# Final scaling of a two-layer encoder trunk: two of the last eight output tiles moved from VectorE to GpSimd

## The reference

```python
def _rmsnorm(x, g):
    xf = x.astype(jnp.float32)
    y = xf * lax.rsqrt(jnp.mean(xf * xf, axis=-1, keepdims=True) + EPS)
    return (y * g.astype(jnp.float32)).astype(x.dtype)
...
        x = x + gate * y
    return _rmsnorm(x, final_g)
```

## Time and profile before

| what | us |
|---|---|
| device time, median of 3 runs (805.86 to 807.53) | 806.22 |
| device time of the profiled execution | 806.58 |
| its span | 804.7 |
| PE busy in it | 793.3 (99%) |
| DVE busy | 654.6 (81%) |
| ACT busy | 459.7 (57%) |
| POOL busy | 86.6 (11%) |

### The profile page before, as it was taken

One profiled execution on the slowest core, in us unless ns is written; L12 is line 12 of the kernel. 1 busy time (PEld: TensorE's weight loads), 2 busy tenths in 40 slices (PEclk: granted clock), 3 DMA queues, 4 the chain that ended last, 5 costly groups with the idle time before them and its releaser, 6 DMA issues.

```text
span 804.7 us, 15186 instructions
## 1 busy us (share of the span) xinstructions
PE 793.3 (99%) x5562; PEld 743.9 (92%) x5562; DVE 654.6 (81%) x952; ACT 459.7 (57%) x642; POOL 86.6 (11%) x112
## 2 busy tenths in 40 slices
PE   8999999999999999999999999989999999999996
PEld 8879999999999999998889888789999999988896
DVE  5989999999999999898896698398888888883334
ACT  4675656565656565572323876656667777762220
POOL 1010000000000000102301242010000000000000
PEclk9999999999999999999999999999999999999999
DMA  9986566666666666679874794655555454454103
GB/s 347 372 205 187 150 183 182 183 182 183 182 182 182 182 182 183 184 262 349 307 236 101 266 223 85 144 149 151 146 156 151 121 145 143 144 182 184 53 1 105
DMA packets 42673, 146.02 MB, mean 181 GB/s; under 512 B 5400, under 2 KB 7702, under 8 KB 42640
## 3 DMA queue, kind: packets, MB, share of 16 engines
q1 hardware_dynamic: 31760, 111.16, 38.5%
q0 software_dynamic: 9728, 32.26, 21.8%
q10 hardware_dynamic: 1152, 2.18, 0.7%
HBM read 109.14 MB, written 4.21 MB: 141 GB/s over the span
## 4 chain that ended last, share of the span: by engine, by line
PE 89%; DMA 4%; DVE 3%; issue 2%; ACT 1%; SPq 0%; POOL 0%; POOLq 0%; DVEq 0%; ACTq 0%
PE pp L1362 11%; PE pp L1363 11%; PE pp L1364 11%; PE pp L1221 8%; PE pp L1222 7%; PE pp L1223 7%; PE p_aux L1362 7%; PE p_aux L1364 7%; PE p_aux L1363 7%; PE pp L1317 2%; PE pp L1494 2%; PE pp L1496 2%; PE pp L1495 2%; PE p_aux L1609 2%; DMA raw_s<-in_stream 1%
## 5 line engine op out<-in xcount | busy, mean ns | idle before, releaser
L1362 PE MATMUL pp<-h_hi,wh 128*128 128x256 f32 x280 | 79.3, 283 | 0.0
L1364 PE MATMUL pp<-h_hi,wl 128*128 128x256 f32 x280 | 79.2, 283 | 0.0
L1363 PE MATMUL pp<-h_lo,wh 128*128 128x256 f32 x280 | 79.2, 283 | 0.0
L826 ACT ACTIVATE wh<-wt 128x1024 fp32r<-128x1024 f32 x56 | 59.0, 1055 | 13.7 <-DVE wt L1899 7.6
L1918 DVE TENSOR_TENSOR wl<-wt,wh 128x1024 fp32r<-128x1024 f32 x56 | 66.5, 1219 | 0.2 <-ACT wh L826 0.2
L1362 PE MATMUL pp<-s_hi,wh 128*128 128x256 f32 x224 | 63.4, 283 | 0.0
L1363 PE MATMUL pp<-s_lo,wh 128*128 128x256 f32 x224 | 63.4, 283 | 0.0
L1364 PE MATMUL pp<-s_hi,wl 128*128 128x256 f32 x224 | 63.4, 283 | 0.0
L1364 PE MATMUL p_aux<-s_hi,wl 128*128 128x256 f32 x224 | 63.4, 283 | 0.0
L1362 PE MATMUL p_aux<-s_hi,wh 128*128 128x256 f32 x224 | 63.4, 283 | 0.0
L1363 PE MATMUL p_aux<-s_lo,wh 128*128 128x256 f32 x224 | 63.4, 283 | 0.0
(11 more groups left out here) (292 smaller groups left out, 2659.1 us busy)
## 6 DMA issues: line engine op xcount, KB each, us to landing
raw<-in_stream SPq DMA_DIRECT2D x140, 512.0 KB, 4.2
wl<-raw POOLq DMA_DIRECT2D x28, 512.0 KB, 4.5
raw_l<-in_stream SPq DMA_DIRECT2D x18, 512.0 KB, 5.9
raw_s<-in_stream SPq DMA_DIRECT2D x16, 512.0 KB, 13.6
wl_b<-raw POOLq DMA_DIRECT2D x16, 512.0 KB, 4.5
raw_m<-in_stream SPq DMA_DIRECT2D x14, 512.0 KB, 3.3
xv_lo<-y POOLq DMA_DIRECT2D x8, 512.0 KB, 6.1
x_s<-in_xt SPq DMA_DIRECT2D x4, 512.0 KB, 5.9
```

Source lines behind the costliest of these rows:

```text
L826: act.activation(wh[g % 2][:, at], wt[g % 2][:, at], ACT.Copy).then_inc(t_hi_cut, 1)
L1362: pe.matmul(out, hi, hi_of(k), start=fresh and k == 0, stop=False, skip_group_check=not fresh)
L1363: pe.matmul(out, hi, lo_of(k), start=False, stop=False, skip_group_check=not fresh)
L1364: mm = pe.matmul(out, lo, hi_of(k), start=False, stop=k == 3, skip_group_check=not fresh)
```

## The change

In the second half, tiles 4 and 5 are no longer scaled by VectorE.

- ScalarE multiplies the second half of tiles 4 and 5 by `final_g` right after `square_x(1, 2)`, in place (two new 128x256 instructions).
- TensorE makes a third broadcast in the second half, 256 columns in one, into another bank of PSUM (`p_pair[1]`). It is issued behind the two that VectorE reads.
- ScalarE copies that bank to SBUF (`rstd_end`), ahead of its stores.
- GpSimd multiplies the two weighted tiles by `rstd_end`, one instruction each.
- VectorE scales six tiles, 0, 1, 2, 3, 6 and 7. SyncE stores 0, 2, 6 and then 4, ScalarE 1, 3, 7 and then 5, still one store a tile.

```diff
+END_POOL = (4, 5)
+END_DVE = (0, 1, 2, 3, 6, 7)
...
+        rstd_end = at_kb("rstd_end", 60, [P, HALF])
...
         @block.sync
-            for k in range(0, KD, 2):
-                sp.wait_ge(out_ready, KD + k + 1)
-                sp.dma_start(out[:, k, halves[1]], x_b[:, k, halves[1]]).then_inc(out_sent, 16)
+            for n in range(0, len(END_DVE), 2):
+                sp.wait_ge(out_ready, KD + n + 1)
+                sp.dma_start(out[:, END_DVE[n], halves[1]], x_b[:, END_DVE[n], halves[1]]).then_inc(out_sent, 16)
+            sp.wait_ge(end_ready, 1)
+            sp.dma_start(out[:, END_POOL[0], halves[1]], x_b[:, END_POOL[0], halves[1]]).then_inc(out_sent, 16)
...
         @block.gpsimd
+            pool.wait_ge(end_weighed, len(END_POOL))
+            pool.wait_ge(end_copied, 1)
+            for n, k in enumerate(END_POOL):
+                pool.tensor_tensor(x_b[:, k, halves[1]], x_b[:, k, halves[1]], rstd_end[:, :], ALU.mult).then_inc(end_ready, 1)
...
         @block.scalar
                 square_x(1, j)
+                for k in range(2 * j, 2 * j + 2):
+                    if k in END_POOL:
+                        act.wait_ge(sq_ready, KD + SQUARES + k + 1)
+                        act.activation(x_b[:, k, halves[1]], x_b[:, k, halves[1]], ACT.Copy,
+                                       scale=cols[:, C_FG + k:C_FG + k + 1]).then_inc(end_weighed, 1)
             cut_hi_late(W_BOUT // 4 + DPAIRS - 1, 0, 1)
             square_half(1, 0)
             square_half(1, 1)
-            for k in range(1, KD, 2):
-                act.wait_ge(out_ready, KD + k + 1)
-                act.dma_start(out[:, k, halves[1]], x_b[:, k, halves[1]]).then_inc(out_sent, 16)
+            act.wait_ge(rstd_bc, 7)
+            act.activation(rstd_end[:, :], p_pair[1][:, 0:HALF], ACT.Copy).then_inc(end_copied, 1)
+            for n in range(1, len(END_DVE), 2):
+                act.wait_ge(out_ready, KD + n + 1)
+                act.dma_start(out[:, END_DVE[n], halves[1]], x_b[:, END_DVE[n], halves[1]]).then_inc(out_sent, 16)
+            act.wait_ge(end_ready, 2)
+            act.dma_start(out[:, END_POOL[1], halves[1]], x_b[:, END_POOL[1], halves[1]]).then_inc(out_sent, 16)
...
         @block.tensor
+            broadcast(p_pair[1][:, 0:HALF], 7, slice(HALF, S))
...
         @block.vector
-                for k in range(KD):
+                for k in range(KD) if half == 0 else END_DVE:
```

More of the change, by code:

```diff
@@ L311, in build @@
         dve_step = sem("dve_step")
+        end_weighed, end_copied, end_ready = sem("end_weighed"), sem("end_copied"), sem("end_ready")
         s_sum, s_hi_cut, s_cut = sem("s_sum"), sem("s_hi_cut"), sem("s_cut")
```

## The result

| what | before | after |
|---|---|---|
| device time, median (7 runs each) | 806.28 | 809.84 |
| lowest and highest run | 805.86 to 807.6 | 809.24 to 810.12 |
| ratio, 95% interval | | 1.0041 (1.003 to 1.0052) |
| profiled execution: device time, span | 806.58, 804.7 | 809.24, 807.4 |

A forecast was written before the change was run, and what follows sets the result against it. The prediction took VectorE's scalings and the DMA engines' stores, level in rate, to bound the last 6 us. Its terms, 0 + 0 + 0 - 0.1 us, took 806.58 to 806.5 profiled, 806.1 as a median; range 805.4 to 807.2.

The forecast's parts named there:

- third rival: Closing barrier: GpSimd's drain is fixed work after its last instruction, ending the kernel 3.3 us later, at 809.5; chance 6%.
- the sum (0 + 0 + 0 - 0.1 us): Whole kernel: weighting, broadcast and copy, and multiplies cost nothing; stores gain 0.1 us, so 806.58 becomes 806.5.
- the 0.3 us of the barrier: End of the kernel: the barrier takes 0.3 us of the 804.7 span after SyncE passes its wait at 804.4.
- The range: Device time from 805.4 to 807.2, said to take in all cases but the drain.
- Weighting: ScalarE behind the square at 772.03: two instructions, 0.84 us, delaying VectorE's cut but hidden by 3.9 us slack; cost nothing.
- a gap: TensorE near 779.7, where its fourth slot is due: a gap there would show the weighting not hidden.
- Broadcast and copy: Last stage: broadcast 799.07 to 799.66, ScalarE's copy 0.38 us to 800.08, fitting before its stores by 0.1 us; cost nothing.
- The multiplies: GpSimd in the last stage: two multiplies at 0.65 us each, 800.12 to 801.4.
- The second rival's exclusion: GpSimd and VectorE exclude each other in the last stage, last issue near 803.0; rival's size 0 to 0.5 us slower, 12%.
- The stores: End of the kernel: last issue moves from 802.52 to 802.1, 0.42 us earlier; 0.05 to 0.1 us of it arrives.
- they would have kept up: First rival, last stores: DMA engines keep up, so the end moves the whole 0.42 us, to 805.8; chance 17%.
- the forecast of no change: Whole kernel: median 806.1 against 806.22, 62% for the forecast; 91% that it measures the same.

The follow-up runs named there:

- E4: The changed kernel with the two multiplies made by VectorE, behind its six tiles, instead of GpSimd: 806.17, ratio 1.0003 to the kernel before.
- E3: The kernel before plus one late two-column memset on GpSimd that nothing waits for: 808.0, ratio 1.0022.
- E1: The changed kernel without GpSimd's drain in the closing barrier: 806.29, ratio 1.0007 to the kernel before.
- E2: The kernel before without GpSimd's drain in the closing barrier: 806.31, ratio 1.0005.
- E10: The changed kernel without GpSimd's drain, storing only 128 of 256 columns of each second-half tile: 805.71, ratio 0.9998 to the kernel before.

## Why the prediction was wrong, by its own steps

**The step that failed is the third rival's chance.** The price and the point from which it decides were right: 3.3 us forecast, 3.46 measured; POOL working past 798.2. I gave it 6% because "its end lies 0.1 us behind SyncE's release at 804.4, which would be a coincidence". It was one. The drain took 6.34 us after GpSimd's last instruction in the kernel before, in the changed one and in E4, 6.32 in E3, whatever SyncE did. In the sum (0 + 0 + 0 - 0.1 us) GpSimd's later end has no term: the 0.3 us of the barrier behind SyncE's wait were carried over, and the runs showed 3.87 us there in the changed kernel. A long sequencer instruction with no visible cause, on the very engine that the change gave new last work, deserved a case inside the range; one coincidence of 0.1 us was the whole argument for leaving it out. The range ended at 807.2, below the lowest run of 809.24.

**The rest held.**

- *Weighting.* VectorE's cut began 3.20 us after the update ahead of it (770.47 to 773.67) instead of 2.40 (771.24 to 773.64), so 0.80 us late for 0.84 forecast, and its idle time behind it shrank from 6.51 to 5.72. TensorE lost nothing by it: E1 is level with E2, and around 779.7, where the prediction looked for a gap, the starts of its matmuls in the changed kernel stay 0.12 us apart. The update before and after:

```profile
771.24 0.75 DVE L2097 SCALAR_TENSOR_TENSOR x_b<-pp,mod,x_b 128x512 f32<-128x512 f32 x1 [1.90 <-PE pp L1223]
```

```profile
770.47 0.75 DVE L2118 SCALAR_TENSOR_TENSOR x_b<-pp,mod,x_b 128x512 f32<-128x512 f32 x1 [1.90 <-PE pp L1243]
```

- *Broadcast and copy.* The copy started 0.43 us after the first scaling, as forecast (799.70 against 799.27), took 0.38, and ScalarE's first store went at 799.40, 0.90 after the first scaling; before it was also 0.90.
- *The multiplies* took 0.72 us each for 0.65 estimated. An estimate of 0.56 us came from the Trainium skill, GPSIMD Engine Reference, section Elementwise side-by-side cycle accounting; the row is longer.
- *The second rival's exclusion.* VectorE's six scalings took 2.44 us, still 0.39 apart, while both multiplies ran beside them. The Trainium skill, SBUF — State Buffer, section Who interferes with whom, says that a VectorE instruction with at most one input in SBUF does not contend with GpSimd: the trace agrees.
- *The stores.* Last issue 0.38 us earlier for 0.42; release 0.03 us earlier for 0.05 to 0.1. The queue after, over 9.9 us from 797.5:

```profile
out_t<-x_b SPq DMA_DIRECT2D x4, 128.0 KB, 1.9
out_t<-x_b ACTq DMA_DIRECT2D x4, 128.0 KB, 2.0
```

The median landing is now 1.9 us on SyncE's queue and 2.0 on ScalarE's instead of 1.8, and the last needs 2.2: what the issues gained, the full DMA engines took back, as their share and E10 show. The estimate from the Trainium skill, DMA: Bandwidth & Descriptors, section Why small descriptors are slow, by which they would have kept up, does not give the rate of these stores.

So with GpSimd's drain taken out (E1, 806.29) the forecast of no change is right, and for its reasons. No version here beats the kernel before: E1, E2 and E4 lie within 0.1% of it, and the last stage is bound by its stores.

## What to carry to other kernels

Before an engine is given new last work, look at what its sequencer still has to do after it: here GpSimd's drain ran 6.34 us beyond its last instruction, and in the kernel before it was hidden with only some 0.05 us to spare. Counted from the first scaling, GpSimd's last instruction ended 3.49 us later after the change, and the kernel 3.46 us later. Taking two tiles off VectorE gained 0.03 us here, since its product leaves through DMA engines that were already full at the same rate. And an instruction of unexplained length near the critical end belongs in the range, however neatly its end fits another event.

## What the runs showed that I had not expected

- GpSimd's drain at the end takes 0.1 us and, up to 76 DMAs, 82 ns for each DMA that GpSimd has issued in the whole program, the last of them issued over 100 us earlier: 4.01 us for 48, 5.32 for 64, 6.30 for 76. The same drain in the opening barrier, before any, took 0.18 us.
- Beyond that it grows less evenly: 6.34 us for 92, 8.95 for 124 with 32 small ones, 7.32 for 124 with 32 wide ones, 10.30 for 156.
- Leaving the drain out took 3.5 us off the changed kernel and nothing off the kernel before. In both, the program waits for GpSimd's DMAs by their semaphores anyway.
